# One product of 512 columns for rounded h and its remainder in the first FFN matrix of block 1

## The chip, the cores and the metric

The kernel runs on one core of one Trainium2 chip. The metric is device time in microseconds (us), the median of several executions. TensorE (PE) multiplies, VectorE (DVE) and ScalarE (ACT) do elementwise work, SyncE (SP) issues the weight transfers, GpSimd (POOL) is idle around the change.

## The reference, cut to what matters

Two blocks run one after the other over 256 tokens of width 1024. Block 1 ends in a gated FFN with `D_FF` = 2816; `w_ffn_in` is the matrix called first here, `w_ffn_out` the second:

```python
h = modulate(rms_norm(x, g_pre_ffn[i]), shift_f, scale_f)
u, gt = jnp.split(h @ w_ffn_in[i], 2, axis=-1)
f = (jax.nn.silu(u) * gt) @ w_ffn_out[i]
x = x + gate_f[:, None, :] * rms_norm(f, g_post_ffn[i])
```

Block 2 (two layers) has four more FFNs, which other code serves and the change leaves alone.

## The kernel before

**Products.** Activations lie transposed, features on the 128 partitions and tokens along the free axis: block 1 works on columns `W1`, 256 of them. To keep fp32 accuracy with rounded (fp32r) operands, every matrix product is three: with each operand split into a rounded part `_hi` and a remainder `_lo`, `tile_mm` (L694 to L700) adds w_hi by h_hi, w_hi by h_lo and w_lo by h_hi in one PSUM tile. Each is its own weight load and a product of 256 columns.

**Panels.** A panel is 16 weight tiles of 128x128 (1 MB) that give two output tiles of 128x256 in `acc`, one of the gate `u` and one of `gt`. The first matrix has 22 panels, numbered t = 0 to 21 below; the second matrix has 8 panels of 22 tiles (2816 columns). All buffers are double, by the parity of the panel: `land` (raw weights, by DMA), `w_hi`, `w_lo`, two banks of `acc`. PE works through one panel in 48 products.

**The ring of a panel.** Once PE has finished panel t (`panel_done`), ACT and DVE evacuate it and prepare the weights of panel t+2 in the same buffers, each engine in the order of its own program:

- ACT, `act_gate_up` (L1318): the sigmoid of `u` out of `acc` (L1323), then `split_hi` of panel t+2 (L662, `w_hi<-land`), then the rounding of the result (L1326, `a_hi<-a_ff`).
- DVE, `dve_gate_up` (L1331): sigmoid by `u` (L1337), that by `gt` (L1339; this frees `acc`), then `split_lo` of panel t+2 (L669, `w_lo<-land,w_hi`), then the remainder `a_lo` (L1345).
- PE starts panel t+2 when its `w_lo` is there and `acc` of that parity is free (`panel_begin`, L689), but not before panel t+1 is streamed.
- SP refills `land` for panel t+4 once `split_lo` has read it.

`section` (L188) writes the code of two panels as the body of a hardware loop for t = 0 to 19, even t first, and t = 20 and 21 once behind it. Panel 0 is written apart on PE, since it takes h tile by tile as it is made. The instruction that loads a function table on ACT (ACT_TABLE_LOAD) is put in by the compiler, not by the source.

Of the kernel before, what the change touches and what calls it, by code (L numbers as in the profile page):

```python
# [14 lines left out]
F32R = mybir.dt.float32r  # L15
ALU = mybir.AluOpType
ACT = mybir.ActivationFunctionType
AX = mybir.AxisListType.X

P = 128  # L20
D = 1024
KT = D // P
SEQ = 256
META = 16
TOK = META + SEQ
# [13 lines left out]
FT = FF // P  # L39
# [18 lines left out]
IN1, AB, OUT, GU, DOWN = 27, 4, 4, 22, 8  # L58
# [129 lines left out]
def section(eng, start, count, fn, loop=0, after=(None, None), unrolled=False):  # L188


    pairs = 0 if unrolled else (count - 2) // 2
    if pairs > 0:
        with eng.Fori(0, pairs) as i:
            for b in range(2):
                fn(i * 2 + b, Panel.of(start + b, loop + i), "same")
    for t in range(2 * max(pairs, 0), count):
        left = count - 1 - t
        fn(t, Panel.of(start + t, loop), "same" if left >= 2 else after[1 - left])
# [6 lines left out]
def allocate(k, nc, ctx):  # L205
# [3 lines left out]
    def at(name, shape, dt=F32, offset=None):  # L209
        size = 4 * int(np.prod(shape[1:]))  # L210
        here = where[0] if offset is None else offset
        t = nc.alloc_sbuf_tensor_at(name, shape, dt, offset=here)
        here += -(-size // 32) * 32
        if offset is None:
            where[0] = here
        return t, here

    def fixed(name, shape, dt=F32):
        return at(name, shape, dt)[0]
# [29 lines left out]
    k.warm = fixed("warm", [P, 8])  # L249
    k.kept = fixed("kept", [P, SHIFT_TILES])  # L250
    h_at = where[0]
    k.h_hi = fixed("h_hi", [P, KT, TOK], F32R)
    k.h_lo = fixed("h_lo", [P, KT, TOK], F32R)
    k.f = fixed("f", [P, KT, TOK])
    h_end = where[0]
    arena = where[0]
# [144 lines left out]
def semaphores(k, sem):  # L401
# [131 lines left out]
    k.meta_zero = sem("meta_zero")  # L533
    k.t1_ready = sem("t1_ready")
    k.a_ready = sem("a_ready")
    k.mix_gates = sem("mix_gates")
    k.chunk_free = sem("chunk_free")
    k.cum_ready = sem("cum_ready")
# [150 lines left out]
def panel_begin(k, pe, p):  # L689
    pe.wait_ge(k.lo_ready, p.count(3))  # L690
    pe.wait_ge(k.acc_free, p.count(1))


def tile_mm(k, out, par, tile, hi, lo, start, stop):  # L694

    c = slice(tile * P, (tile + 1) * P)
    mm = k.nc.tensor.matmul
    mm(out, k.w_hi[:, par, c], hi, start=start, stop=False)  # L698
    mm(out, k.w_hi[:, par, c], lo, start=False, stop=False)  # L699
    return mm(out, k.w_lo[:, par, c], hi, start=False, stop=stop)  # L700
# [48 lines left out]
def pe_project(k, pe, start, count, tiles, W, loop=0, ready=None):  # L749

    n = W.stop - W.start

    def one(i, p, _):
        panel_begin(k, pe, p)
        for o in range(tiles):
            for t in range(KT):
                last = tile_mm(k, k.acc[:, 2 * p.par + o, 0:n], p.par, o * KT + t, k.h_hi[:, t, W],
                               k.h_lo[:, t, W], t == 0, t == KT - 1)  # L760
        last.then_inc(k.panel_done, 1)
    peeled = 0
    if ready is not None:
        p = Panel.of(start, loop)
        panel_begin(k, pe, p)
        for t in range(KT):
            pe.wait_ge(ready[0], ready[1] + (t + 1))
            for o in range(tiles):
                last = tile_mm(k, k.acc[:, 2 * p.par + o, 0:n], p.par, o * KT + t, k.h_hi[:, t, W],
                               k.h_lo[:, t, W], t == 0, t == KT - 1)  # L770
        last.then_inc(k.panel_done, 1)
        peeled = 1
    section(pe, start + peeled, count - peeled, one, loop)

# [465 lines left out]

def act_gate_up_z(k, act, i, start, W, nxt, loop=0):

    z = i - 1
    a = k.nc.scalar.activation

    def rounded(t):
        act.wait_ge(k.a_ready, z * FT + (t + 1))
        a(k.a_hi[:, t, W], k.a_ff[:, t % 2, W], ACT.Copy).then_inc(k.ah_ready, 1)  # L1250

    def sigmoid(t):
        act.wait_ge(k.t1_ready, z * FT + (t + 1))
        a(k.sig[:, t % 2, W], k.t_ff[:, t % 2, W], ACT.Sigmoid).then_inc(k.sig_ready, 1)  # L1254
    for t in range(GU):
        p = Panel.of(start + t, loop)
        if t == GU - 1:
            sigmoid(t)
            split_hi(k, act, p.ahead2(), nxt)
            rounded(t - 1)  # L1260
            rounded(t)
            continue
        if t > 0:
            split_hi(k, act, p.ahead2(), GU_K if t < GU - 2 else nxt)
        sigmoid(t)
        if t > 0:
            rounded(t - 1)


def dve_gate_up_z(k, dve, b, i, start, W, nxt, loop=0):  # L1270

    n = W.stop - W.start
    v = k.nc.vector
    c = k.scale[:, W]
    z = i - 1

    def scaled(t, p):
        dve.wait_ge(k.panel_done, p.count(3))
        v.tensor_tensor(k.t_ff[:, t % 2, W], k.acc[:, 2 * p.par, 0:n], c, ALU.mult).then_inc(k.t1_ready, 1)  # L1279
        v.tensor_tensor(k.g_ff[:, t % 2, W], k.acc[:, 2 * p.par + 1, 0:n], c, ALU.mult).then_inc(k.acc_free, 1)  # L1280

    def product(t):
        dve.wait_ge(k.sig_ready, i * FT + (t + 1))
        v.tensor_tensor(k.t_ff[:, t % 2, W], k.sig[:, t % 2, W], k.t_ff[:, t % 2, W], ALU.mult)
        dve.drain()
        v.tensor_tensor(k.a_ff[:, t % 2, W], k.t_ff[:, t % 2, W], k.g_ff[:, t % 2, W],  # L1286
                        ALU.mult).then_inc(k.a_ready, 1)

    def rest(t):
        dve.wait_ge(k.ah_ready, i * FT + (t + 1))  # L1290
        v.tensor_tensor(k.a_lo[:, t, W], k.a_ff[:, t % 2, W], k.a_hi[:, t, W].bitcast(F32),  # L1291
                        ALU.subtract).then_inc(k.al_ready, 1)
    for t in range(GU):
        p = Panel.of(start + t, loop)
        scaled(t, p)
        if t > 0:
            product(t - 1)
        if t == GU - 1:
            dve.drain()
            rest(t - 2)  # L1300
            dve.drain()
            product(t)
            rest(t - 1)
            split_lo(k, dve, p.ahead2(), nxt)
            rest(t)
            continue
        if t > 0:
            split_lo(k, dve, p.ahead2(), GU_K if t < GU - 2 else nxt)
        if t > 1:
            rest(t - 2)  # L1310
        if t in (2, 3):
            dve_undo_root(k, W, t - 2)
        if 4 <= t < 4 + KT:
            dve_undo(k, W, t - 4)
        dve.drain()


def act_gate_up(k, act, i, start, W, nxt, loop=0):  # L1318
    n = W.stop - W.start

    def one(t, p, ahead_size):
        act.wait_ge(k.panel_done, p.count(3))
        k.nc.scalar.activation(k.sig[:, p.par, W], k.acc[:, 2 * p.par, 0:n], ACT.Sigmoid).then_inc(k.sig_ready, 1)  # L1323
        ahead(split_hi, k, act, p, ahead_size, GU_K)
        act.wait_ge(k.acc_free, p.count(3))
        k.nc.scalar.activation(k.a_hi[:, bass.ds(t, 1), W].rearrange("p a n -> p (a n)"), k.a_ff[:, p.par, W],  # L1326
                               ACT.Copy).then_inc(k.ah_ready, 1)
    section(act, start, GU, one, loop, nxt)


def dve_gate_up(k, dve, i, start, W, nxt, loop=0):  # L1331
    n = W.stop - W.start
    v = k.nc.vector

    def one(t, p, ahead_size):
        dve.wait_ge(k.sig_ready, i * FT + (t + 1))
        v.tensor_tensor(k.t_ff[:, p.par, W], k.sig[:, p.par, W], k.acc[:, 2 * p.par, 0:n], ALU.mult)  # L1337
        dve.drain()
        v.tensor_tensor(k.a_ff[:, p.par, W], k.t_ff[:, p.par, W], k.acc[:, 2 * p.par + 1, 0:n],  # L1339
                        ALU.mult).then_inc(k.acc_free, 1)  # L1340
        ahead(split_lo, k, dve, p, ahead_size, GU_K)
        dve.drain()
        dve.wait_ge(k.ah_ready, i * FT + (t + 1))
        a = bass.ds(t, 1)
        v.tensor_tensor(k.a_lo[:, a, W].rearrange("p a n -> p (a n)"), k.a_ff[:, p.par, W],  # L1345
                        k.a_hi[:, a, W].rearrange("p a n -> p (a n)").bitcast(F32),
                        ALU.subtract).then_inc(k.al_ready, 1)
    section(dve, start, GU, one, loop, nxt)
# [29 lines left out]
def pe_ffn(k, pe, i, pre, gu, down, W, nxt, loop=0):  # L1378
    if i == 0:
        pe_pre(k, pe, pre, W)  # L1380
        pe_project(k, pe, gu, GU, 2, W, loop, ready=(k.hl_ready, pre * KT))
    else:
        pe_project_z(k, pe, pre - 1, gu, GU, 2, W, loop)
    pe_down(k, pe, down, W, i * FT, loop)
    if nxt is None:
        pe_stat(k, pe, pre, W)
    else:
        pe_stat_z(k, pe, pre, down, 1, W, loop)
# [2010 lines left out]
```

## Time and profile before

| | |
|---|---|
| Median of 3 runs | 2059.01 us (2057.66 to 2059.4) |
| The profiled execution | 2057.19 us, its span 2055.3 us |
| PE busy | 1923.9 us, 94% |
| DVE busy | 1404.2 us, 68% |
| ACT busy | 908.6 us, 44% |
| First FFN matrix of block 1 | starts at 534.25 us, the second at 662.23 us of the span |

The span runs from the first to the last instruction of the profiled execution. Busy shares are means over the whole program; the stretch that the change touches is some 128 us of it. A product lasts some 280 ns by its record, but products overlap: what counts is the time from the start of one to the start of the next.

### The profile page before, as it was taken

Reading aid. Unit: us, or ns where it says so; the run is one execution under the profiler, and the core shown is the slowest. Engines: PE = TensorE matmul, PEld = TensorE weight load, DVE = VectorE, ACT = ScalarE, POOL = GpSimd, SP = SyncE. Lnnn points to the kernel's source line nnn. Section 1 sums busy time; section 2 is a strip of 40 time slices with the busy share of each in tenths; the row PEclk is TensorE's granted clock in tenths of the full one; section 3 lists DMA queues with packets and bytes.
Section 4 is the critical chain, followed back from the end, with each engine's and each line's share of the span. In section 5 each row is a group of like instructions: output and inputs, shape, how many; then the busy total and the mean of one; then the engine's idle time right before and its main releaser. Section 6 shows DMA issues by size and latency. Waiting matters only on the chain.

```text
span 2055.3 us, 36364 instructions
## 1 busy us (share of the span) xinstructions
PE 1923.9 (94%) x14822; PEld 1869.1 (91%) x14822; DVE 1404.2 (68%) x2171; ACT 908.6 (44%) x1347; POOL 100.4 (5%) x164
## 2 busy tenths in 40 slices
PE   7897889999799999999999999999999989999997
PEld 7896689988799989998999999999999889889997
DVE  6996576777766477745767777747774676677764
ACT  3443443444455444434555444434443455444442
POOL 0201031100000000002100000000000200000000
PEclk7998998989899999999999999999999999999999
DMA  9684110004355435543333535543554323353552
GB/s 354 254 307 142 42 62 1 1 1 163 106 185 206 180 128 181 187 155 122 103 110 117 172 136 174 186 173 128 179 187 158 130 90 124 112 196 128 187 199 102
DMA packets 41720, 301.42 MB, mean 147 GB/s; under 512 B 4544, under 2 KB 6736, under 8 KB 7808
## 3 DMA queue, kind: packets, MB, share of 16 engines
q1 hardware_dynamic: 41008, 296.90, 41.0%
q0 software_dynamic: 592, 2.87, 0.4%
q8 instruction: 82, 1.34, 0.3%
q14 instruction: 38, 0.31, 0.0%
HBM read 298.70 MB, written 1.05 MB: 146 GB/s over the span
## 4 chain that ended last, share of the span: by engine, by line
PE 76%; DVE 13%; DVEq 4%; ACT 3%; DMA 2%; issue 1%; POOL 0%; SPq 0%; ACTq 0%; POOLq 0%
PE acc L698 20%; PE acc L700 19%; PE acc L699 19%; DVE w_lo L669 3%; ACT w_hi L662 1%; PE mb L721 1%; PE acc L2052 1%; PE mb L2052 1%; DVEq L845 1%; DMA land<-in_w_in 1%; PE acc L2725 1%; DVE upd L794 1%; DMA ada_first<-in_w_ada 1%; DVE gla_sq L3063 1%; PE mb L2049 1%
## 5 line engine op out<-in xcount | busy, mean ns | idle before, releaser
L698 PE MATMUL acc<-h_hi,w_hi 128*128 128x272 f32 (+1 forms) x2960 | 871.6, 294 | 43.9 <-DVE w_lo L669 19.4
L700 PE MATMUL acc<-h_hi,w_lo 128*128 128x272 f32 (+1 forms) x2960 | 854.1, 289 | 0.0
L699 PE MATMUL acc<-h_lo,w_hi 128*128 128x272 f32 (+1 forms) x2960 | 852.7, 288 | 0.0
L669 DVE TENSOR_TENSOR w_lo<-land,w_hi 128x2048 fp32r<-128x2048 f32 (+1 forms) x239 | 576.1, 2411 | 169.4 <-ACT w_hi L662 168.8
L662 ACT ACTIVATE w_hi<-land 128x2048 fp32r<-128x2048 f32 (+1 forms) x239 | 479.3, 2006 | 479.2 <-PE acc L700 412.8
L698 PEld LDWEIGHTS acc<-h_hi,w_hi 128*128 128x128 f32 x2960 | 568.5, 192 | 57.5 <-DVE w_lo L669 23.2
L699 PEld LDWEIGHTS acc<-h_lo,w_hi 128*128 128x128 f32 x2960 | 568.3, 192 | 2.1 <-issue 0.2
L700 PEld LDWEIGHTS acc<-h_hi,w_lo 128*128 128x128 f32 x2960 | 568.4, 192 | 0.0
L698 PE MATMUL acc<-a_hi,w_hi 128*128 128x272 f32 (+1 forms) x880 | 251.8, 286 | 0.7 <-DVE w_lo L669 0.5
L699 PE MATMUL acc<-a_lo,w_hi 128*128 128x272 f32 (+1 forms) x880 | 250.3, 284 | 0.0
L700 PE MATMUL acc<-a_hi,w_lo 128*128 128x272 f32 (+1 forms) x880 | 250.2, 284 | 0.0
L698 PEld LDWEIGHTS acc<-a_hi,w_hi 128*128 128x128 f32 x880 | 165.3, 188 | 1.4 <-DVE w_lo L669 0.9
L699 PEld LDWEIGHTS acc<-a_lo,w_hi 128*128 128x128 f32 x880 | 165.9, 189 | 0.0
L700 PEld LDWEIGHTS acc<-a_hi,w_lo 128*128 128x128 f32 x880 | 165.6, 188 | 0.0
L1279 DVE TENSOR_TENSOR t_ff<-acc,ssum 128x272 f32<-128x272 f32 (+1 forms) x88 | 38.5, 437 | 85.0 <-PE acc L700 82.8
L1123 ACT ACTIVATE sq_post<-acc 128x272 f32<-128x272 f32 (+1 forms) x48 | 18.0, 393 | 175.7 <-PE acc L700 175.7
L1148 DVE TENSOR_SCALAR f<-acc,vec 128x272 f32<-128x272 f32 (+1 forms) x40 | 19.9, 497 | 65.3 <-ACT sq_post L1123 64.4
L2502 DVE TENSOR_TENSOR p<-acc,ssum 128x272 f32<-128x272 f32 (+1 forms) x56 | 24.2, 433 | 42.4 <-PE acc L700 41.9
L2634 POOL MEMSET sel<- 128x1024 f32 x2 | 1.9, 948 | 1028.4 <-PE acc L709 1028.4
L1254 ACT ACTIVATE sig<-t_ff 128x272 f32<-128x272 f32 (+1 forms) x88 | 36.2, 411 | 25.7 <-DVE t_ff L1279 25.7
L1286 DVE TENSOR_TENSOR a_ff<-t_ff,g_ff 128x272 f32<-128x272 f32 (+1 forms) x88 | 38.6, 439 | 7.3 <-issue 0.9
L1291 DVE TENSOR_TENSOR a_lo<-a_ff,a_hi 128x272 fp32r<-128x272 f32 (+1 forms) x88 | 37.9, 431 | 2.3 <-ACT a_hi L1250 1.9
(555 smaller groups left out, 2561.4 us busy)
## 6 DMA issues: line engine op xcount, KB each, us to landing
land<-in_w_gu SPq DMA_DIRECT2D x110, 1024.0 KB, 4.8
land<-in_w_in SPq DMA_DIRECT2D x65, 1024.0 KB, 4.9
land<-in_w_down SPq DMA_DIRECT2D x40, 1408.0 KB, 6.0
ada_first<-in_w_ada SPq DMA_DIRECT2D x24, 1024.0 KB, 8.7
land<-in_w_ab SPq DMA_DIRECT2D x12, 1024.0 KB, 5.0
land<-in_w_out SPq DMA_DIRECT2D x12, 1024.0 KB, 4.8
land<-in_w_in_single SPq DMA_DIRECT2D x6, 512.0 KB, 3.5
const<-in_const POOLq DMA_DIRECT2D x1, 1134.0 KB, 11.1
```

What stands on the lines that cost most here:

```text
L662: k.nc.scalar.activation(k.w_hi[:, p.par, 0:size * P], k.land[:, p.par, 0:size * P], ACT.Copy).then_inc(k.hi_ready, 1)
L669: k.nc.vector.tensor_tensor(k.w_lo[:, p.par, 0:size * P], k.land[:, p.par, 0:size * P], k.w_hi[:, p.par, 0:size * P].bitcast(F32), ALU.sub ...
L698: mm(out, k.w_hi[:, par, c], hi, start=start, stop=False)
L699: mm(out, k.w_hi[:, par, c], lo, start=False, stop=False)
L700: return mm(out, k.w_lo[:, par, c], hi, start=False, stop=stop)
L721: r = k.nc.tensor.matmul(k.mb[:, 2, 0:n], k.mean_ones[:, :], moving, start=done == 0, stop=done == KT)
L1254: a(k.sig[:, t % 2, W], k.t_ff[:, t % 2, W], ACT.Sigmoid).then_inc(k.sig_ready, 1)
L1279: v.tensor_tensor(k.t_ff[:, t % 2, W], k.acc[:, 2 * p.par, 0:n], c, ALU.mult).then_inc(k.t1_ready, 1)
L1286: v.tensor_tensor(k.a_ff[:, t % 2, W], k.t_ff[:, t % 2, W], k.g_ff[:, t % 2, W], ALU.mult).then_inc(k.a_ready, 1)
L1291: v.tensor_tensor(k.a_lo[:, t, W], k.a_ff[:, t % 2, W], k.a_hi[:, t, W].bitcast(F32), ALU.subtract).then_inc(k.al_ready, 1)
L2052: last = mm(bank[:, 1, c * P + lo:c * P + hi], m["x_bd"][:, c, :], m["xr"][:, c, lo:hi], start=True, stop=True)
L2502: k.nc.vector.tensor_tensor(chunk_tile(k, l, c), k.acc[:, 2 + o, 0:W.stop - W.start], k.scale[:, W], ALU.mult).then_inc((k.chunk_free, k.a ...
```

## The change

In the first matrix of block 1's FFN, `h_hi` and `h_lo` become two halves of one tensor `k.h`, and PE takes both in one product with w_hi: 512 columns, which fill a whole PSUM bank. The product of w_lo by h_hi stays, into the first half of the bank. The weight w_hi is loaded once instead of twice. The two halves of the bank are added at evacuation: ACT copies the second halves of both tiles to `sq_post`, DVE adds them to the first halves, giving `t_ff` (u) and `g_ff` (gt), and the sigmoid and the two multiplications then read these from SBUF. `a_ready` is a counter that was used by the other FFNs; their counts are moved on by one FFN.

```diff
-    k.h_hi = fixed("h_hi", [P, KT, TOK], F32R)
-    k.h_lo = fixed("h_lo", [P, KT, TOK], F32R)
+    k.h = fixed("h", [P, 2, KT, TOK], F32R)
+    k.h_hi, k.h_lo = k.h[:, 0, :, :], k.h[:, 1, :, :]
...
+def pe_project_wide(k, pe, start, count, W, ready):
+    n = W.stop - W.start
+    mm = k.nc.tensor.matmul
+    def products(p, o, t):
+        c = slice((o * KT + t) * P, (o * KT + t + 1) * P)
+        both = k.acc[:, 2 * p.par + o, 0:2 * n].rearrange("p (a n) -> p a n", a=2)
+        mm(both, k.w_hi[:, p.par, c], k.h[:, :, t, W], start=t == 0, stop=False)
+        return mm(k.acc[:, 2 * p.par + o, 0:n], k.w_lo[:, p.par, c], k.h_hi[:, t, W], start=False, stop=t == KT - 1)
+    def one(i, p, _):
+        panel_begin(k, pe, p)
+        for o in range(2):
+            for t in range(KT):
+                last = products(p, o, t)
+        last.then_inc(k.panel_done, 1)
...
 def act_gate_up(k, act, i, start, W, nxt, loop=0):
...
         act.wait_ge(k.panel_done, p.count(3))
-        k.nc.scalar.activation(k.sig[:, p.par, W], k.acc[:, 2 * p.par, 0:n], ACT.Sigmoid).then_inc(k.sig_ready, 1)
+        k.nc.scalar.activation(k.sq_post[:, 2 * p.par:2 * p.par + 2, 0:n], k.acc[:, 2 * p.par:2 * p.par + 2, n:2 * n],
+                               ACT.Copy).then_inc(k.part_ready, 1)
+        act.wait_ge(k.t1_ready, t + 1)
+        k.nc.scalar.activation(k.sig[:, p.par, W], k.t_ff[:, p.par, W], ACT.Sigmoid).then_inc(k.sig_ready, 1)
         ahead(split_hi, k, act, p, ahead_size, GU_K)
-        act.wait_ge(k.acc_free, p.count(3))
+        act.wait_ge(k.a_ready, t + 1)
...
 def dve_gate_up(k, dve, i, start, W, nxt, loop=0):
...
+        dve.wait_ge(k.part_ready, t + 1)
+        part = k.sq_post[:, 2 * p.par:2 * p.par + 2, 0:n]
+        v.tensor_tensor(k.t_ff[:, p.par, W], k.acc[:, 2 * p.par, 0:n], part[:, 0, :], ALU.add).then_inc(k.t1_ready, 1)
+        v.tensor_tensor(k.g_ff[:, p.par, W], k.acc[:, 2 * p.par + 1, 0:n], part[:, 1, :], ALU.add).then_inc(k.acc_free, 1)
         dve.wait_ge(k.sig_ready, i * FT + (t + 1))
-        v.tensor_tensor(k.t_ff[:, p.par, W], k.sig[:, p.par, W], k.acc[:, 2 * p.par, 0:n], ALU.mult)
+        v.tensor_tensor(k.t_ff[:, p.par, W], k.sig[:, p.par, W], k.t_ff[:, p.par, W], ALU.mult)
         dve.drain()
-        v.tensor_tensor(k.a_ff[:, p.par, W], k.t_ff[:, p.par, W], k.acc[:, 2 * p.par + 1, 0:n],
-                        ALU.mult).then_inc(k.acc_free, 1)
+        v.tensor_tensor(k.a_ff[:, p.par, W], k.t_ff[:, p.par, W], k.g_ff[:, p.par, W],
+                        ALU.mult).then_inc(k.a_ready, 1)
```

What this makes of two engines' programs is seen in the compiled order of their instructions. First ACT, the body of the loop, from the top to the second panel; `sig` is the sigmoid, `w_hi` the rounded weights of panel t+2. Before:

```order
L1323 ACT_TABLE_LOAD
L1323 ACTIVATE sig<-acc 128x256 [waits panel_done]
L660 ISA
L661 ISA [waits landed1]
L662 ACTIVATE w_hi<-land 128x2048 [waits panel_done]
L1326 ISA [waits acc_free]
L1326 ACTIVATE a_hi<-a_ff 128x256
L1322 REGISTER_ALU
L1323 ACTIVATE sig<-acc 128x256 [waits panel_done]
```

In the changed kernel the same place reads:

```order
L1352 ACT_TABLE_LOAD
L1352 ACTIVATE sq_post<-acc 128x2x256 [waits panel_done]
L1354 ISA
L1355 ACT_TABLE_LOAD
L1355 ACTIVATE sig<-t_ff 128x256 [waits t1_ready]
L661 ISA
L662 ISA [waits landed1]
L663 ACTIVATE w_hi<-land 128x2048 [waits panel_done]
L1358 ISA [waits a_ready]
L1358 ACTIVATE a_hi<-a_ff 128x256
L1351 REGISTER_ALU
L1352 ACTIVATE sq_post<-acc 128x2x256 [waits panel_done]
```

There is one more table load in the body, between the copy and the sigmoid of the first (even) panel; the second (odd) panel of the body and the two panels behind the loop have none.

Then DVE, one panel of its loop body; `w_lo` is what PE waits for. Before:

```order
L1337 TENSOR_TENSOR t_ff<-sig,acc 128x256 [waits sig_ready]
L1339 TENSOR_TENSOR a_ff<-t_ff,acc 128x256
L668 ISA
L669 TENSOR_TENSOR w_lo<-land,w_hi 128x2048 [waits hi_ready]
L1345 ISA [waits ah_ready]
L1345 TENSOR_TENSOR a_lo<-a_ff,a_hi 128x256
```

In the changed kernel:

```order
L1370 TENSOR_TENSOR t_ff<-acc,sq_post 128x256 [waits part_ready]
L1371 TENSOR_TENSOR g_ff<-acc,sq_post 128x256
L1373 TENSOR_TENSOR t_ff<-sig,t_ff 128x256 [waits sig_ready]
L1375 TENSOR_TENSOR a_ff<-t_ff,g_ff 128x256
L669 ISA
L670 TENSOR_TENSOR w_lo<-land,w_hi 128x2048 [waits hi_ready]
L1381 ISA [waits ah_ready]
L1381 TENSOR_TENSOR a_lo<-a_ff,a_hi 128x256
```

Two additions stand ahead of the two multiplications, and the first of them stands between ACT's copy and ACT's sigmoid.

## Rows read from the trace of the kernel before

**Rows 1.** The page, part 4: share of the chain that ended last, by engine.

```profile
PE 76%; DVE 13%; DVEq 4%; ACT 3%; DMA 2%; issue 1%; POOL 0%; SPq 0%; ACTq 0%; POOLq 0%
```

**Rows 2.** Busy us of each engine by stage: first panel, and panels 1 to 20.

```profile
core 0: us, PE busy (x) PEld busy (x) DVE busy (x) ACT busy (x) POOL busy (x), PEclk, DMA share, GB/s
532.00:542.00 10.00, 7.75 (x45) 7.78 (x46) 7.08 (x17) 5.24 (x9) 0.00 (x0) 0.66 0.23 93
545.00:655.00 110.00, 110.00 (x932) 110.00 (x931) 69.76 (x77) 58.98 (x67) 0.00 (x0) 1.00 0.53 185
```

**Rows 3.** Timeline of ACT over two panels: start us, us, what, [idle before].

```profile
548.30 0.39 ACT L1323 ACTIVATE sig<-acc 128x256 f32<-128x256 f32 x1 [3.18 <-PE acc L700]
548.58 1.91 ACT L662 ACTIVATE w_hi<-land 128x2048 fp32r<-128x2048 f32 x1
550.39 0.40 ACT L1326 ACTIVATE a_hi<-a_ff 128x256 f32 x1
550.81 1.28 ACT L1323 ACT_TABLE_LOAD   x1
553.98 0.38 ACT L1323 ACTIVATE sig<-acc 128x256 f32<-128x256 f32 x1 [1.89 <-PE acc L700]
```

**Rows 4.** Timeline of DVE over the first of these panels.

```profile
548.72 0.42 DVE L1337 TENSOR_TENSOR t_ff<-sig,acc 128x256 f32<-128x256 f32 x1 [0.92 <-ACT sig L1323]
549.22 0.42 DVE L1339 TENSOR_TENSOR a_ff<-t_ff,acc 128x256 f32<-128x256 f32 x1
550.52 2.29 DVE L669 TENSOR_TENSOR w_lo<-land,w_hi 128x2048 fp32r<-128x2048 f32 x1 [0.88 <-ACT w_hi L662]
553.04 0.43 DVE L1345 TENSOR_TENSOR a_lo<-a_ff,a_hi 128x256 f32 x1 [0.22 <-issue]
```

**Rows 5.** Timeline where the first matrix ends and the second begins, three engines.

```profile
656.22 0.38 ACT L1323 ACTIVATE sig<-acc 128x256 f32<-128x256 f32 x1 [3.19 <-PE acc L700]
656.50 2.55 ACT L662 ACTIVATE w_hi<-land 128x2816 fp32r<-128x2816 f32 x1
...
659.09 3.09 DVE L669 TENSOR_TENSOR w_lo<-land,w_hi 128x2816 fp32r<-128x2816 f32 x1 [1.53 <-ACT w_hi L662]
...
661.58 0.28 PE L700 MATMUL acc<-h_hi,w_lo 128*128 128x256 f32 x1
661.90 0.39 ACT L1323 ACTIVATE sig<-acc 128x256 f32<-128x256 f32 x1 [2.55 <-PE acc L700]
...
662.23 0.38 PE L698 MATMUL acc<-a_hi,w_hi 128*128 128x256 f32 x1 [0.37 <-DVE w_lo L669]
...
662.45 0.28 PE L699 MATMUL acc<-a_lo,w_hi 128*128 128x256 f32 x1
```

**Rows 6.** Busy us and count of PE: second matrices, products of 256 and 272 columns.

```profile
680.00:720.00 40.00, 40.00 (x341) 1.00 0.51 191
880.00:920.00 40.00, 40.00 (x322) 1.00 0.44 158
```

**Rows 7.** Groups of ACT by line and shape: busy us, mean ns, idle before.

```profile
L1323 ACT ACT_TABLE_LOAD x10 | 12.8, 1283 | 0.2
...
L1254 ACT ACTIVATE sig<-t_ff 128x256 f32<-128x256 f32 x22 | 8.8, 399 | 6.3 <-DVE t_ff L1279 6.3
...
L1402 ACT ACTIVATE qkv<-acc 128x512 f32 x6 | 3.5, 580 | 0.0
```

**Rows 8.** Timeline of ACT in block 2, a table load between two instructions.

```profile
976.03 1.92 ACT L662 ACTIVATE w_hi<-land 128x2048 fp32r<-128x2048 f32 x1 [2.71 <-PE acc L700]
977.97 1.28 ACT L2538 ACT_TABLE_LOAD   x1
979.26 0.43 ACT L2538 ACTIVATE lf<-lf 8x272 f32<-8x272 f32 x1
```

**Rows 9.** Timeline of PE, one panel start of the program's first stage.

```profile
60.47 0.39 PE L698 MATMUL acc<-h_hi,w_hi 128*128 128x256 f32 x1 [1.29 <-DVE w_lo L669]
```

**Rows 10.** Busy us, count and granted clock of PE in that stage.

```profile
55.00:115.00 60.00, 50.43 (x420) 1.00 0.70 262
```

More of the change, by code:

```diff
@@ L535, in semaphores @@
     k.a_ready = sem("a_ready")
+    k.part_ready = sem("part_ready")
     k.mix_gates = sem("mix_gates")
@@ L773, in pe_project @@
     section(pe, start + peeled, count - peeled, one, loop)
+def pe_project_wide(k, pe, start, count, W, ready):
[12 more added lines that the diff above has]
+        last.then_inc(k.panel_done, 1)
+    p = Panel.of(start)
+    panel_begin(k, pe, p)
+    for t in range(KT):
+        pe.wait_ge(ready[0], ready[1] + (t + 1))
+        for o in range(2):
+            last = products(p, o, t)
+    last.then_inc(k.panel_done, 1)
+    section(pe, start + 1, count - 1, one)
 def dve_ada(k, dve, n, src):
@@ L1243, in act_gate_up_z @@
 def act_gate_up_z(k, act, i, start, W, nxt, loop=0):
-    z = i - 1
     a = k.nc.scalar.activation
     def rounded(t):
-        act.wait_ge(k.a_ready, z * FT + (t + 1))
+        act.wait_ge(k.a_ready, i * FT + (t + 1))
         a(k.a_hi[:, t, W], k.a_ff[:, t % 2, W], ACT.Copy).then_inc(k.ah_ready, 1)
     def sigmoid(t):
-        act.wait_ge(k.t1_ready, z * FT + (t + 1))
+        act.wait_ge(k.t1_ready, i * FT + (t + 1))
         a(k.sig[:, t % 2, W], k.t_ff[:, t % 2, W], ACT.Sigmoid).then_inc(k.sig_ready, 1)
@@ L1274, in dve_gate_up_z @@
     c = k.scale[:, W]
-    z = i - 1
     def scaled(t, p):
@@ L1380, in pe_ffn @@
         pe_pre(k, pe, pre, W)
-        pe_project(k, pe, gu, GU, 2, W, loop, ready=(k.hl_ready, pre * KT))
+        pe_project_wide(k, pe, gu, GU, W, (k.hl_ready, pre * KT))
     else:
```

## The prediction

> **What bounds the kernel now.** I read the chain that ended last first: PE holds 76% of it [rows 1], so the question is whether PE is also what ends last in this stage. The table by stage says yes: over panels 1 to 20 PE is busy 110.00 of 110.00 us at a granted clock of 1.00, which is its level of 2.4 GHz, while DVE is busy 69.76 and ACT 58.98 us [rows 2]. 932 products in 110 us are 118 ns from start to start. Sigmoids of successive panels start 5.68 us apart [rows 3], and 48 products of 118 ns are 5.66 us.
>
> The busy shares suggest much room on ACT and DVE. The timelines tell how much of it lies on the path, and it is little, because the weights of panel t+2 are made behind the evacuation of panel t. Counting from A, the start of ACT's first instruction after a panel: the sigmoid occupies ACT to 0.28, w_hi to 2.19, w_lo runs from 2.22 to 4.51 [rows 3, 4]. PE takes up new weights 0.05 us after w_lo (it ends at 662.18, PE starts at 662.23 [rows 5]), so panel t+2 could begin at A+4.56. PE gets to it when it has streamed panel t+1. The last product of a panel starts at 661.58, the next could start 0.12 later at 661.70, and ACT sees the panel done at 661.90 [rows 5]: a panel ends for PE at A-0.20, and the next at A+5.48. So 5.48 - 4.56 = 0.92 us is all the cover that the ring has per panel. Where the preparation is longer, for the 2816 columns of the second matrix, it is already exceeded: PE idles from 661.70 to 662.23.
>
> **Part by part.** *PE.* Per weight tile three products of 256 columns become one of 512 and one of 256. No row shows a back-to-back stream of 512 columns at fp32r, so I bound it. 40.00 us hold 341 products of 256 columns and 322 of 272 [rows 6], 117.3 and 124.2 ns, so 16 columns cost 6.9 ns, 0.43 per column; from 118 ns, 256 more columns give 228 ns. At least it takes 512/2.4 = 213 ns, at most two products, 236. A panel is then 16 x (118+228) = 5.54 us, between 5.30 and 5.66: 0.14 us less than 5.68, some 3.1 us in 22 panels if PE stays the bound. Panel 0 runs at a granted clock of 0.66 [rows 2] and I leave it as it is.
>
> The Trainium skill, page "TensorE: Matmul & The Clock Gate", section "Wait — 56ns, not 53.3ns?", gives a warm gap of N/2.4 + about 2.5 ns, which would be 109 and 216 ns; the rows have 118 at 256 columns, so the measurement decides here. By the page's gaps a panel would be 5.20 us, and the sum below about 3.4 us lower.
>
> *The ring.* Ahead of w_hi there now stand a copy of 512 elements (0.58 us, as qkv<-acc of 512 [rows 7]), an addition (0.42, as the DVE operations with one operand in PSUM [rows 4]), and the sigmoid, now from SBUF (0.40 [rows 7]; its successor still starts 0.28 after it). Handovers between engines take 0.02 to 0.03 us [rows 3, 4]. And in even panels of the loop ACT has a table load between copy and sigmoid: 1.28 us, the same for all ten of them before [rows 7]. Before, the one load of the loop stood ahead of the wait and ran in ACT's idle time, from 550.81 to 552.09 with the sigmoid at 553.98 [rows 3]; the one at the top of the new loop lies there too. The new one does not: it waits for the copy. It runs beside the addition, which it outlasts.
>
> Odd panels: copy 0.58, +0.02, add 0.42, +0.03, sigmoid 0.28, w_hi 1.91, +0.03, w_lo 2.29, +0.05: PE could start at A+5.61. Even panels: copy 0.58, +0.02, load 1.28, +0.02, 0.28, 1.91, +0.03, 2.29, +0.05 = A+6.46. PE arrives at A-0.20+5.54 = A+5.34. Both are late, and the even ones by 1.12 us: the cover is gone and the ring takes over as the bound.
>
> *What follows for a pair of panels.* An even panel t starts at S. After a pause the first product takes 0.10 us more (662.23 to 662.45 against 118 ns [rows 5]), so it ends at S+5.64, A is S+5.84, and panel t+2 starts at S+5.84+6.46 = S+12.30. Before, a pair took 2 x 5.68 = 11.36. The odd ring must fit in between: panel t+1 starts at S+5.64, its A is S+11.38, its copy is done at 11.96, but DVE is held by the even panel until a_lo is done, 0.23+0.43 after w_lo [rows 4], at S+12.91. From there add, sigmoid, w_hi and w_lo take 5.0 us, to S+17.9, and PE arrives from panel t+2 at 12.30+5.64 = 17.94. So the odd ring just hides behind the even one and adds nothing. On ACT the loop's first load ends near S+17.2, ahead of the next copy at 12.30+5.84 = 18.1.
>
> *The sum.* Panel 2 starts at A+6.46 instead of A+5.48 behind the same panel 0: +0.98. Nine pairs bring PE from panel 2 to panel 20: 9 x 0.94 = +8.46. Panel 20 has no load but 2816 columns: its chain is 0.58+0.02+0.42+0.03+0.28+2.55+0.03+3.09+0.05 = 7.05 [rows 5], so the second matrix starts 5.64+0.20+7.05 = 12.89 after panel 20 starts; before it was 650.34 to 662.23, 11.89: +1.00. Together +10.4 us. Its first panel (66 products, 7.8 us) covers panel 21's chain as it does now. Nothing behind it changes but its start. The profiled execution goes from 2057.2 to 2067.6 us; the median of the runs lies 1.8 above that execution, so I forecast 2069.4.
>
> *Free edits.* The second addition, the multiplications (now from SBUF) and a_hi lie beside w_hi or w_lo. acc is free after the additions, long before w_lo. The transfer for panel t+4 is issued behind w_lo, later than now by the same 2 us as the w_hi that needs it. The moved counts and the joined tensor cost nothing.
>
> **Rivals.**
>
> 1. *The load hides* (not slower). If the second load ran ahead of panel_done, or cost next to nothing because its table is there, even panels would be as odd ones: 5.54+0.20+5.61 = 11.35 us per panel pair on the ring, as now, and only the +1.0 at the second matrix stays: 2060. It decides once the load is over before the addition, 0.46 us behind the copy. Against it: the compiled order puts it behind the copy on an engine that works in order, and all ten loads before fetch the table for the same sigmoid again and take 1283 ns.
>
> 2. *PE stays the bound* (faster). Then 22 panels give 3.1 us, up to 8.4 at 5.30 us each, less 1.0: 2051 to 2057. It needs a ring under A+5.34 in all panels; even the odd one is 0.27 over it.
>
> 3. *A fast 512-column stream.* If the wide product took hardly longer than one of 256 columns, a panel would be 16 x (118+118) = 3.78 us, and the ring of an even pair 3.78+0.10+0.20+6.46 = 10.54. But ACT and DVE alone need, from one odd w_hi to the next, 0.40+1.28+0.58+1.28+0.28+1.91 on ACT, then 2.29+0.23+0.43+0.42+0.28+1.91 across both, with handovers 11.4 us, as long as a pair now. So about 2060. Against it: 0.43 ns per column in [rows 6] leaves no room for it. The Trainium skill has such a figure, page "TensorE: Matmul & The Clock Gate", section "Back-to-back issue gap": 131 ns sustained at N=512, by which an estimate of the panel is 3.98 us and the end the same.
>
> 4. *A dearer switch.* If the load held ACT for twice its recorded 1.28 us, each of ten even chains would grow by as much: 12.8 us more, 2082. Against it: in block 2 a load starts 0.03 us after the instruction ahead of it ends, and the next starts 1.29 behind the load's start [rows 8]. The Trainium skill, page "ScalarE: Activation LUTs", section "What ACT_TABLE_LOAD costs", has 1283 ns and a drain of 1380, 2.66 us together; by it an estimate is 2083, and the trace shows the first part but no drain.
>
> 5. *The clock falls in the new pauses.* PE would pause about 1.1 us once in 12. The first stage of the program pauses 1.29 us ahead of a panel, by the same kind of wait [rows 9], is busy only 50.43 of 60 us, and was granted 1.00 throughout [rows 10]. So I give this little; one stretch at half the clock would double a panel, 5 us.
>
> **How the numbers follow.** Forecast 0.83; rival 1 0.08, 2 0.03, 3 0.02, 4 and 5 0.02 each. The length of a panel counts ten times in the sum: 5.30 takes 2.4 off, 5.66 adds 1.2. The 0.10 at a pause, if it is not there, takes 1.0 off. Register and wait handling that the trace of before doesn't show in this place may add 0.1 per chain, 1.1. That is +7.0 to +12.7, 2066.0 to 2071.7; with the 1.7 us over which the runs spread, 2064.5 to 2073. The rivals hold 0.17 and stay outside. What a measurement here can tell from no change is about 0.2%, 4.1 us: slower 0.87 (forecast, 4, 5), within it 0.10 (1 and 3), faster 0.03.
>
> **What would show it.** Products of 512 columns near 228 ns apart; a table load directly behind the copy in every second panel, ending some 0.85 us after the addition; ACT's first instructions in turn 5.5 and 6.8 us apart, 12.3 per pair; PE idle about 1.1 us ahead of each even panel, ended by w_lo; clock 1.00. A regular 5.7 us with the load elsewhere would prove rival 1, PE without pauses rival 2. I would also be wrong if the odd chain, hidden by only a few hundredths, sets its own pace.

## The result, and the profile after

| | before | changed | ratio, 95% interval |
|---|---|---|---|
| Median, 6 runs each | 2058.81 us (2052.59 to 2060.43) | 2073.11 us (2069.01 to 2075.2) | 1.0072 [1.0056, 1.0088] |
| The profiled execution | 2057.19 us, span 2055.3 | 2069.01 us, span 2067.1 | |

The changed kernel is slower, as forecast, by 14.3 us where 10.4 were forecast; 2073.11 lies 0.1 us above the upper end of the range. The two profiled executions lie 11.8 us apart.

The stage of the change is bounded by the ring of a panel now. This is the table by stage for panels 1 to 20 in the changed kernel, with the columns of [rows 2]: PE no longer fills it (100.60 of 110.00 us), though the granted clock is 1.00.

```profile
545.00:655.00 110.00, 100.60 (x565) 86.13 (x565) 75.92 (x106) 77.16 (x89) 0.00 (x0) 1.00 0.48 163
```

PE's timeline there (start us, us, what, [idle before]) shows a pause of about 1.0 us ahead of every even panel, ended by w_lo, and inside a panel the stream of wide and narrow products: 560.97 and 573.42 are two starts of even panels, 12.45 us apart. The last row is the first product of the second matrix.

```profile
560.97 0.49 PE L788 MATMUL acc<-h,w_hi 128*128 128x512 f32 x1 [1.04 <-DVE w_lo L670]
561.30 0.28 PE L789 MATMUL acc<-h,w_lo 128*128 128x256 f32 x1
561.42 0.39 PE L788 MATMUL acc<-h,w_hi 128*128 128x512 f32 x1
561.64 0.28 PE L789 MATMUL acc<-h,w_lo 128*128 128x256 f32 x1
561.76 0.39 PE L788 MATMUL acc<-h,w_hi 128*128 128x512 f32 x1
...
573.42 0.49 PE L788 MATMUL acc<-h,w_hi 128*128 128x512 f32 x1 [1.02 <-DVE w_lo L670]
...
673.65 0.38 PE L699 MATMUL acc<-a_hi,w_hi 128*128 128x256 f32 x1 [1.59 <-DVE w_lo L670]
```

ACT and DVE of the same pair answer to [rows 3] and [rows 4]. First ACT, from the copy of an even panel (566.83) to that of the odd one (572.43); the first row is the copy of panel 0.

```profile
541.90 0.60 ACT L1352 ACTIVATE sq_post<-acc 128x512 f32<-128x512 f32 x1 [1.39 <-PE acc L789]
...
566.83 0.60 ACT L1352 ACTIVATE sq_post<-acc 128x512 f32<-128x512 f32 x1 [1.14 <-PE acc L789]
567.44 1.28 ACT L1355 ACT_TABLE_LOAD   x1
568.74 0.42 ACT L1355 ACTIVATE sig<-t_ff 128x256 f32<-128x256 f32 x1
569.06 1.90 ACT L663 ACTIVATE w_hi<-land 128x2048 fp32r<-128x2048 f32 x1
570.87 0.40 ACT L1358 ACTIVATE a_hi<-a_ff 128x256 f32 x1
572.43 0.60 ACT L1352 ACTIVATE sq_post<-acc 128x512 f32<-128x512 f32 x1 [1.17 <-PE acc L789]
574.30 0.42 ACT L1355 ACTIVATE sig<-t_ff 128x256 f32<-128x256 f32 x1 [1.27 <-DVE t_ff L1370]
```

```profile
567.46 0.42 DVE L1370 TENSOR_TENSOR t_ff<-acc,sq_post 128x256 f32<-128x256 f32 x1 [0.40 <-ACT sq_post L1352]
567.80 0.41 DVE L1371 TENSOR_TENSOR g_ff<-acc,sq_post 128x256 f32<-128x256 f32 x1
569.19 0.42 DVE L1373 TENSOR_TENSOR t_ff<-sig,t_ff 128x256 f32<-128x256 f32 x1 [0.97 <-ACT sig L1355]
...
571.00 2.29 DVE L670 TENSOR_TENSOR w_lo<-land,w_hi 128x2048 fp32r<-128x2048 f32 x1 [0.88 <-ACT w_hi L663]
573.51 0.42 DVE L1381 TENSOR_TENSOR a_lo<-a_ff,a_hi 128x256 f32 x1 [0.22 <-issue]
573.85 0.42 DVE L1370 TENSOR_TENSOR t_ff<-acc,sq_post 128x256 f32<-128x256 f32 x1
```

What to see: the load begins 0.01 us after the copy and ends at 568.72, the addition beside it is over at 567.88, so the load alone holds the sigmoid for 0.84 us. w_lo of the even panel ends at 573.29, PE starts 0.13 us behind it. And the odd panel's copy, done at 573.03, waits for DVE until 573.85, which is why ACT idles 1.27 us ahead of the odd sigmoid. The chains and the pauses are those that were forecast; their sizes are taken up below.

For what follows I use one measure, the stretch from ACT's first evacuation instruction (end of panel 0) to the first product of the second matrix: 662.23 - 542.64 = 119.59 us before, 673.65 - 541.90 = 131.75 after, +12.16. Panel 0 is left out of it because its length hangs on when the clock rises: the granted clock goes from 0.50 to 1.00 near 539.7 us of the span before and near 537.9 here, and panel 0 takes 8.39 us before, 7.45 here, 8.34 in the next execution of the same kernel. In the stretch it is 1.00 in all ten traces.

### The profile page after: what moved, and what is told of

Read it like the earlier page. It is cut to its first block, busy times and chain, and to the rows that moved or that the text cites. A ratio compares the mean times of both kernels' runs of the same rounds, so it can differ in the third digit from the quotient of the medians.

```text
span 2067.1 us, 35756 instructions
## 1 busy us (share of the span) xinstructions
PE 1927.5 (93%) x14470; PEld 1853.7 (90%) x14470; DVE 1419.5 (69%) x2215; ACT 935.1 (45%) x1379; POOL 102.7 (5%) x164
## 4 chain that ended last, share of the span: by engine, by line
PE 74%; DVE 14%; ACT 4%; DVEq 4%; issue 2%; DMA 1%; POOL 0%; ACTq 0%; SPq 0%; POOLq 0%
PE acc L699 18%; PE acc L701 17%; PE acc L700 17%; DVE w_lo L670 4%; ACT w_hi L663 2%; PE acc L788 2%; PE mb L722 1%; PE acc L789 1%; PE mb L2088 1%; PE acc L2088 1%; DVEq L876 1%; PE acc L2761 1%; DVE gla_sq L3099 1%; DVE upd L825 1%; PE mb L2085 1%
## 5 line engine op out<-in xcount | busy, mean ns | idle before, releaser
L699 PE MATMUL acc<-h,w_hi 128*128 128x272 f32 (+1 forms) x2608 | 772.1, 296 | 38.8 <-DVE w_lo L670 18.8
L701 PE MATMUL acc<-h,w_lo 128*128 128x272 f32 (+1 forms) x2608 | 754.0, 289 | 0.0
L700 PE MATMUL acc<-h,w_hi 128*128 128x272 f32 (+1 forms) x2608 | 752.8, 289 | 0.0
L699 PEld LDWEIGHTS acc<-h,w_hi 128*128 128x128 f32 x2608 | 500.9, 192 | 52.2 <-DVE w_lo L670 22.5
L700 PEld LDWEIGHTS acc<-h,w_hi 128*128 128x128 f32 x2608 | 501.1, 192 | 2.0 <-issue 0.2
L701 PEld LDWEIGHTS acc<-h,w_lo 128*128 128x128 f32 x2608 | 500.8, 192 | 0.0
L788 PE MATMUL acc<-h,w_hi 128*128 128x512 f32 x352 | 125.9, 399 | 14.7 <-DVE w_lo L670 10.4
L789 PE MATMUL acc<-h,w_lo 128*128 128x256 f32 x352 | 99.4, 282 | 0.0
L788 PEld LDWEIGHTS acc<-h,w_hi 128*128 128x128 f32 x352 | 66.9, 190 | 33.1 <-issue 17.0
L789 PEld LDWEIGHTS acc<-h,w_lo 128*128 128x128 f32 x352 | 66.9, 190 | 0.0
```

Source lines behind the costliest of these rows:

```text
L788: mm(both, k.w_hi[:, p.par, c], k.h[:, :, t, W], start=t == 0, stop=False)
L789: return mm(k.acc[:, 2 * p.par + o, 0:n], k.w_lo[:, p.par, c], k.h_hi[:, t, W], start=False, stop=t == KT - 1)
```

## The experiments

The stretches of all eight runs are in this table, and their times against runs of the kernel before on the same chip: 2057.35 us in 25 runs for "changed, again", "load ahead of the panel", "wide product taken apart" and "skewed order, wide product", 2057.91 in 22 runs for the other four.

| kernel | stretch, us | median, us (runs) | ratio, 95% interval |
|---|---|---|---|
| changed, again | 131.88 | 2068.57 (6) | 1.0049 [1.0035, 1.0063] |
| changed, third time | 131.79 | 2069.61 (6) | 1.0054 [1.0036, 1.0072] |
| load ahead of the panel | 123.60 | 2060.46 (12) | 1.0019 [1.0007, 1.0031] |
| wide product taken apart | 132.52 | 2068.89 (8) | 1.0048 [1.0031, 1.0064] |
| before, with the load alone | 126.74 | 2063.98 (9) | 1.0022 [1.0005, 1.0040] |
| PE's panels written out | 131.10 | 2073.17 (4) | 1.0076 [1.0056, 1.0096] |
| skewed order, wide product | 117.95 | 2055.91 (12) | 0.9998 [0.9983, 1.0012] |
| skewed order, three products | 119.81 | 2056.09 (12) | 0.9997 [0.9981, 1.0014] |

### Is the load in the ring the largest part?

The changed kernel with a sigmoid of one element per partition ahead of the wait, in `act_gate_up`, so that the load moves there:

```diff
     def one(t, p, ahead_size):
+        if p.par == start % 2:
+            k.nc.scalar.activation(k.warm[:, 0:1], k.eps[:, 0:1], ACT.Sigmoid)
         act.wait_ge(k.panel_done, p.count(3))
```

> The changed kernel with a sigmoid of one element per partition on ACT at the head of each pair of panels, ahead of the wait for the panel, so that the table is loaded there and no load stands between copy and sigmoid. Theory (the load in the even ring is the largest part): even and odd panels go alike, a ring of 5.86 + 5.78 = 11.6 us per pair against 12.47 in the changed kernel and 11.36 before; the stage takes 131 to 133 us, and the time is 3 to 5 us over before. Rival (copy and addition in the ring are the cause, the load hides behind them): the stage stays within 1 us of 139.2.

ACT's timeline in this kernel: the load and the small sigmoid end at 570.99, before the panel is done at 571.93, and copy and sigmoid are 1.08 us apart instead of 1.91.

```profile
569.50 1.28 ACT L1352 ACT_TABLE_LOAD   x1
570.79 0.20 ACT L1352 ACTIVATE warm<-eps 128x1 f32<-128x1 f32 x1
571.93 0.60 ACT L1354 ACTIVATE sq_post<-acc 128x512 f32<-128x512 f32 x1 [0.93 <-PE acc L789]
573.01 0.42 ACT L1357 ACTIVATE sig<-t_ff 128x256 f32<-128x256 f32 x1 [0.49 <-DVE t_ff L1372]
```

A pair takes 11.66 us (571.93 after 560.27) where 11.6 were expected, the stretch falls from 131.75 to 123.60; with panel 0 it is 131.98 us, inside 131 to 133, and the time is 3.1 us over before. Of the 12.2 us the load makes 8.2; copy and addition in the ring, less what the shorter stream gives back, make the other 4.0. Even and odd panels, which I had expected to go alike, do not quite: PE still pauses 0.2 us ahead of each even panel in the loop and ahead of no odd one. The rival, that the load hides, is refuted.

The counterpart adds a copy of one element per partition to the kernel before, in `act_gate_up`, and with it the load:

```diff
         act.wait_ge(k.panel_done, p.count(3))
+        if p.par == start % 2:
+            k.nc.scalar.activation(k.warm[:, 0:1], k.acc[:, 2 * p.par, 0:1], ACT.Copy)
         k.nc.scalar.activation(k.sig[:, p.par, W], k.acc[:, 2 * p.par, 0:n], ACT.Sigmoid).then_inc(k.sig_ready, 1)
```

> The kernel before, with three products and its own evacuation, and one thing added: in even panels a copy of one element per partition behind the wait for the panel, which makes the compiler put its second table load between that copy and the sigmoid. Theory: the load alone takes the ring over the bound. The even ring is 0.20+0.02+1.28+0.02+0.28+1.91+0.03+2.29+0.13 = 6.16 us, a pair 5.68+0.10+0.20+6.16 = 12.14, and from the end of panel 0 to the second matrix 127 to 128 us against 119.6 before and 131.8 with the change. Rival (the load is hidden or cheap in this place): below 121 us.

ACT's timeline and PE's start behind it, in that kernel:

```profile
566.33 0.17 ACT L1324 ACTIVATE warm<-acc 128x1 f32<-128x1 f32 x1 [2.62 <-PE acc L700]
566.51 1.28 ACT L1325 ACT_TABLE_LOAD   x1
567.80 0.38 ACT L1325 ACTIVATE sig<-acc 128x256 f32<-128x256 f32 x1
```

```profile
572.45 0.38 PE L698 MATMUL acc<-h_hi,w_hi 128*128 128x256 f32 x1 [0.47 <-DVE w_lo L669]
```

A pair is 12.06 us (566.33 to 578.39) and the stretch 126.74, 0.3 below the expected 127 to 128 and 7.2 over before. One table load, with 0.18 us of the small copy ahead of it, in an otherwise unaltered ring costs more than half of what the whole change costs.

### Does the wide product itself gain anything?

In the changed kernel the wide product was taken apart, with everything else as it is:

```diff
-        both = k.acc[:, 2 * p.par + o, 0:2 * n].rearrange("p (a n) -> p a n", a=2)
-        mm(both, k.w_hi[:, p.par, c], k.h[:, :, t, W], start=t == 0, stop=False)
+        bank = k.acc[:, 2 * p.par + o, :]
+        mm(bank[:, 0:n], k.w_hi[:, p.par, c], k.h_hi[:, t, W], start=t == 0, stop=False)
+        mm(bank[:, n:2 * n], k.w_hi[:, p.par, c], k.h_lo[:, t, W], start=False, stop=False)
```

> The changed kernel with the wide product taken apart again: w_hi by h_hi into the first half of the bank and w_hi by h_lo into the second, 256 columns each, w_hi loaded twice; evacuation as in the changed kernel. Theory (the ring is the bound, a panel's streaming counts once per pair): a panel streams 5.68 instead of 5.56 us, a pair 12.6 us, the stage 1 to 1.6 us over 139.2. Rival (the wide product saves its 0.12 us in both panels of a pair): 2.5 us or more over 139.2. If the wide product is itself slower than two, the stage falls below 139.2.

Its even copies, from ACT's timeline, are 12.55 us apart, 0.08 more than the mean of the changed kernel's pairs in the loop (12.47):

```profile
556.66 0.60 ACT L1353 ACTIVATE sq_post<-acc 128x512 f32<-128x512 f32 x1 [1.25 <-PE acc L790]
...
569.21 0.60 ACT L1353 ACTIVATE sq_post<-acc 128x512 f32<-128x512 f32 x1 [1.25 <-PE acc L790]
```

The stretch grew by 0.77 us, a little less than the expected 1 to 1.6: the product's gain of some 0.08 us per panel counts once per pair. Where PE is the bound it should count twice. For that ACT and DVE were written out in another order (the core of it):

```diff
-        act.wait_ge(k.t1_ready, t + 1)
-        k.nc.scalar.activation(k.sig[:, p.par, W], k.t_ff[:, p.par, W], ACT.Sigmoid).then_inc(k.sig_ready, 1)
-        ahead(split_hi, k, act, p, ahead_size, GU_K)
-        act.wait_ge(k.a_ready, t + 1)
-        k.nc.scalar.activation(k.a_hi[:, bass.ds(t, 1), W].rearrange("p a n -> p (a n)"), k.a_ff[:, p.par, W],
-                               ACT.Copy).then_inc(k.ah_ready, 1)
+        split_hi(k, act, p.ahead2(), GU_K if t < GU - 2 else nxt[0])
+        act.wait_ge(k.t1_ready, t + 1)
+        a(k.sig[:, t % 2, W], k.t_ff[:, t % 2, W], ACT.Sigmoid).then_inc(k.sig_ready, 1)
+        if t > 0:
+            rounded(t - 1)
...
+        summed(t, p)
+        if t > 0:
+            product(t - 1)
...
+        split_lo(k, dve, p.ahead2(), GU_K if t < GU - 2 else nxt[0])
+        if t > 1:
+            rest(t - 2)
```

> The wide product, with ACT and DVE in another order, written out for all 22 panels: ACT copies, makes w_hi of panel t+2, then takes the sigmoid of t and rounds the result of t-1; DVE adds, multiplies for t-1, makes w_lo, then the remainder of t-2. The ring is then copy, w_hi, w_lo: 0.60+0.02+1.90+0.04+2.29+0.13 = 4.98 us after a panel, under the 5.36 at which PE arrives. Theory: PE is the bound again at 5.56 us per panel, the stage takes 125 to 126.5 us, 1.5 to 3 us less than before, and the time is 0 to 3 us under before. Rival (the wide product saves nothing where PE is the bound): stage 128 us or more.

PE's table for 105 us of this kernel has no pause, and copies follow each other every 5.59 us; the single table load of the written-out code stands at 543.20 us, in the evacuation of panel 0. With panel 0 the stage is 126.32 us, inside the expected 125 to 126.5.

```profile
545.00:650.00 105.00, 105.00 (x603) 1.00 0.55 189
```

```profile
563.12 0.60 ACT L1358 ACTIVATE sq_post<-acc 128x512 f32<-128x512 f32 x1 [2.57 <-PE acc L789]
568.71 0.60 ACT L1358 ACTIVATE sq_post<-acc 128x512 f32<-128x512 f32 x1 [2.58 <-PE acc L789]
```

The same order with the wide product taken apart as above:

> The order of ACT and DVE that took load and sigmoid out of the ring (117.95 us from the end of panel 0 to the second matrix), with the wide product taken apart into two of 256 columns. Theory: PE is the bound in both, so here the wide product counts in every panel: 5.68 instead of 5.59 us, the stretch 119.8 to 120.3. Rival (the gain of 1.6 us came from the order and not from the product): 118 to 118.5.

Its copies are 5.68 us apart:

```profile
555.43 0.60 ACT L1359 ACTIVATE sq_post<-acc 128x512 f32<-128x512 f32 x1 [2.67 <-PE acc L790]
561.11 0.60 ACT L1359 ACTIVATE sq_post<-acc 128x512 f32<-128x512 f32 x1 [2.67 <-PE acc L790]
```

The stretch is 117.95 with the wide product against 119.81 without, 1.86 us or 0.09 per panel (21 panels lie in it): this is what the product gains where the ring is shorter than a panel. The times of both kernels can't be told from before, since 1.6 us is 0.08%. The skewed order with the wide product is the shortest stretch of all, and no more than that is shown.

### Where are the missing microseconds?

The changed kernel was run twice more:

> The changed kernel once more, unaltered. In the one profiled execution of it the first FFN matrix of block 1 takes 139.20 us from its first product to that of the second matrix, 11.2 more than before (127.98), but the medians of the runs lie 14.3 us apart. Theory: the ring of a panel is the whole cause and the rest of the 14.3 is scatter between executions, so the stage is again 139.2 within 0.3 and the time lies 11 to 13 us over before. Rival: the pauses of PE bring the clock down in some executions; then a stage is some 3 to 7 us longer in one of them and the times stay 14 us or more over before.

> The changed kernel a third time, unaltered. Two sets of six runs put it at 2073.1 and 2068.6, +14.3 and +11.2 us over before, while the stretch from the end of panel 0 to the second matrix is longer by 12.2 us in both traces. Theory: the change costs the 12.2 us of this stretch and the sets differ by scatter of stages that the change does not touch (clock); a third set then lies 10 to 14.5 us over before, and the stretch is 131.8 within 0.2. Rival: the changed kernel has a further cost of 2 us or more outside this stretch; then the set lies 14 us or more over before, and so does the mean of all.

The stretch is 131.88 and 131.79; the rival (clock lost in the new pauses) finds nothing in three traces, where the granted clock of the stretch is 1.00. With panel 0 the second execution's stage was 140.22, outside the 139.2 within 0.3 that I had expected: the difference is panel 0, which took 8.34 us there instead of 7.45 because the granted clock rose from 0.50 later. The times were +11.2 and +11.7 us, so the +14.3 did not come back. Over 18 runs of the changed kernel the median is 2069.8, over 53 of the kernel before 2057.7: +12.1, as much as the stretch.

The last question was the 1.7 us by which the stretch exceeds the sum:

```diff
-    section(pe, start + 1, count - 1, one)
+    section(pe, start + 1, count - 1, one, unrolled=True)
```

> The changed kernel with PE's 21 panels written out instead of a loop, so that PE waits for w_lo by a constant and not by a register; ACT and DVE unaltered. Of the 12.2 us, 10.4 were forecast, and the largest part of the gap is the handover from w_lo to PE, 0.13 us in the loop against the 0.05 that was put in from a row outside a loop. Theory (the register wait is what costs it): handover 0.05, pair 12.39 instead of 12.47, the stretch 130.8 to 131.1. Rival (the handover is as long whatever the wait): 131.8.

DVE's w_lo here ends at 561.66, and PE starts 0.06 us later:

```profile
559.37 2.29 DVE L670 TENSOR_TENSOR w_lo<-land,w_hi 128x2048 fp32r<-128x2048 f32 x1 [0.88 <-ACT w_hi L663]
```

```profile
561.72 0.50 PE L788 MATMUL acc<-h,w_hi 128*128 128x512 f32 x1 [0.97 <-DVE w_lo L670]
574.12 0.50 PE L788 MATMUL acc<-h,w_hi 128*128 128x512 f32 x1 [0.96 <-DVE w_lo L670]
```

In the loop it was 0.13 (573.29 to 573.42). A pair is 12.40, the stretch 131.10, 0.65 of the 1.7 us less: as the theory of the register wait has it. The changed kernel shows the same within itself: PE's loop ends with panel 18, and panel 20, written behind it, starts 0.06 us after its w_lo (660.55 to 660.61).

```profile
658.26 2.29 DVE L670 TENSOR_TENSOR w_lo<-land,w_hi 128x2048 fp32r<-128x2048 f32 x1 [0.88 <-ACT w_hi L663]
```

```profile
660.61 0.50 PE L788 MATMUL acc<-h,w_hi 128*128 128x512 f32 x1 [0.97 <-DVE w_lo L670]
```

Whether it is the register's value or something else that a loop brings, no run separates. The median of the written-out kernel is the highest of all although its stretch is shorter than the changed kernel's, in 4 runs; the next section returns to it.

## Why the prediction was right in its way and too low in size

**The mechanism held at each step.** PE was the bound; copy, load and sigmoid took the ring over its cover; even panels pause, the odd ring hides behind them; the granted clock stayed at 1.00 through pauses of 1.0 us. The 512-column product was put at 228 ns and takes about that (wide and narrow together 0.34 to 0.35 us, where 0.346 was put). Rival 1 fell with the moved load, 2 with PE's pauses, 3 with the spacing of the products. Rival 4 fell too: the sigmoid starts 1.30 us after the load starts, with no drain behind it.

**The term that was mis-sized is the even ring**, A+6.46 in the text and 6.59 in the trace (566.83 to 573.42). By its pieces: copy and its handover 0.61 for 0.60, load 1.30 for 1.30, sigmoid 0.32 for 0.28, w_hi 1.94 for 1.94, w_lo with PE's start 2.42 for 2.34. The two errors have one kind: a duration taken from a row in another setting. 0.28 was the sigmoid out of PSUM [rows 3]; out of SBUF w_hi follows it 0.32 later. 0.05 was the handover at the second matrix [rows 5], outside a loop; in the loop it is 0.13, and the written-out PE shows that this is the difference. With 0.02 to 0.03 more per panel, a pair is 12.46 instead of 12.30: 0.13 + 9 x 0.16 + 0.15 = 1.7 us in all. So the stretch was lengthened by 12.2 us, inside the +7.0 to +12.7 of the sum, but only because that also held 1.2 for a longer panel: the 1.1 put for waits is less than the 1.7 that were missing. With the 1.7 the forecast would have been 2071.2.

**The range's other part failed too**: the 1.7 us that I gave to scatter between executions, from three runs. Of the 3.9 us between +10.4 and +14.3, 1.7 are the stretch and some 2.1 lie outside it. (The range was also rounded inward: 2066.0 - 1.7 and 2071.7 + 1.7 are 2064.3 and 2073.4, and 2073.11 lies inside that.) Runs of the kernel before lie between 2048.93 us, at a mean granted clock of 0.961, and 2068.37, at 0.951. The stages that no kernel here alters vary by themselves. PE's table from the second matrix to the end, the same instructions in both kernels (the load alone, then skewed with three products):

```profile
668.89:2067.40 1398.51, 1340.85 (x10442) 0.97 0.43 150
```

```profile
658.21:2047.90 1389.69, 1333.68 (x10442) 0.98 0.43 150
```

1398.5 against 1389.7 us, with the lower granted clock in the longer one; in ten traces this rest lies between these two, and the start up to the end of panel 0 between 537.0 and 544.6. So a median of six runs can be off by 2 to 3 us for reasons that the change does not touch: the same kernel gave +14.3, +11.2 and +11.7. Where the first set had its extra 2.1 us is not shown: only its lowest execution has a trace, and the granted clocks of its runs, 0.955 to 0.960 and once 0.909, are but for that one those of the two later sets (0.955 to 0.961). The written-out PE's 2073.17 may be of this kind, which is not shown either: its profiled execution had 1395.2 us behind the stretch, that of the changed kernel 1393.4, and its four runs have the low granted clocks of 0.953 to 0.955. What sets the clock in a given execution stays open.

## What to carry to other kernels

An engine that is half idle can still have no time to give: here the ring through ACT and DVE had 0.92 us of cover per panel while their busy shares were 63% (DVE) and 54% (ACT). Before adding to an evacuation, write the chain from the end of one tile to the start of the one that reuses its buffers, and look in the compiled order for table loads that slip into it; a small instruction of the right function at the head of the loop moves such a load out of the way. And take handovers from rows with the same kind of wait, and scatter from many runs or from stages that stay the same.

## What the runs showed that I had not expected

In a loop, where it waits by a register, PE starts 0.13 to 0.14 us after the end of w_lo; in written-out code, where it waits by a constant, 0.05 to 0.06. On ACT w_hi starts 0.28 us after a sigmoid with its input in PSUM, also where a load stands right ahead of that sigmoid, and 0.32 after one with its input in SBUF. And unaltered stages of 1390 us vary by 8.8 us between executions, some 70% of the 12.2 us under study.
